# Weighted latent of an absorbed-MLA attention: plain fp32 matmuls on whole probabilities in place of three fp32r matmuls on high and low parts

## The reference, cut to what matters

```python
q_l = jnp.concatenate([qn_l, apply_axial_rope(qp_l, rope)], axis=-1)
kv = (rms_norm(c_kv, g_kva) @ w_kvup).reshape(b, t, MLA_HEADS, QK_NOPE + V_DIM)
s = jnp.einsum('bqhd,bkhd->bhqk', q, k).astype(jnp.float32) * scale
p = jax.nn.softmax(s, axis=-1).astype(v.dtype)
return jnp.einsum('bhqk,bkhd->bqhd', p, v)
```

## Time and profile before

| | |
|---|---|
| median of 3 runs | 2826.54 us (2825.86 to 2827.65) |
| time of the profiled execution | 2825.79 us |
| its span in the profile | 2823.7 us |
| TensorE busy | 2639.9 us (93%) |
| granted TensorE clock, mean | 0.972 of full speed |
| attention stage, from the first transposes to the last `weighted_values` | about 1872 to 2329 us of the span |
| one head of it | 58.3 to 58.4 us |

### The profile page before, as it was taken

One profiled execution on the slowest core, in us unless ns is written; L12 is line 12 of the kernel. 1 busy time (PEld: TensorE's weight loads), 2 busy tenths in 40 slices (PEclk: granted clock), 3 DMA queues, 4 the chain that ended last, 5 costly groups with the idle time before them and its releaser, 6 DMA issues.

```text
span 2823.7 us, 33170 instructions
## 1 busy us (share of the span) xinstructions
PE 2639.9 (93%) x12374; PEld 2131.7 (75%) x12374; DVE 1283.3 (45%) x1610; ACT 737.3 (26%) x979; POOL 638.8 (23%) x360
## 2 busy tenths in 40 slices
PE   7978888999999899999999989989999999899997
PEld 4856665777878688888888877878888887677776
DVE  5653444775123543134313565246666664522243
ACT  4133333000111222011101123146566651211120
POOL 2200110333333233333333332200000003222221
PEclk9979998999999999999999989999999999999998
DMA  4100001543112111111111111100000002000011
GB/s 149 45 27 19 30 31 47 181 167 125 46 71 82 33 52 45 52 45 49 48 64 48 52 54 38 45 23 9 7 15 7 8 9 76 30 30 30 30 41 71
DMA packets 40399, 143.27 MB, mean 51 GB/s; under 512 B 4972, under 2 KB 6252, under 8 KB 39950
## 3 DMA queue, kind: packets, MB, share of 16 engines
q1 hardware_dynamic: 35724, 124.03, 13.1%
q10 hardware_dynamic: 4610, 18.35, 1.8%
HBM read 135.81 MB, written 6.55 MB: 50 GB/s over the span
## 4 chain that ended last, share of the span: by engine, by line
PE 76%; DVE 11%; issue 6%; ACT 4%; DMA 2%; DVEq 0%; ACTq 0%; SPq 0%
PE PS L437 58%; PE PS L828 3%; PE PS L768 3%; PE PS L800 2%; PE PS L776 2%; DMA AW<-in_ada 2%; ACT E L1236 1%; PE PS L478 1%; PE PS L927 1%; PE PS L923 1%; DVE cols L1850 1%; PE PS L470 1%; DVE H L1422 1%; DVE SA L1550 1%; ACT SA L1042 1%
## 5 line engine op out<-in xcount | busy, mean ns | idle before, releaser
L437 PE MATMUL PS<-H,w_hl 128*128 128x512 f32 x6624 | 1549.6, 395 | 65.3 <-DVE H L1422 16.6
L437 PEld LDWEIGHTS PS<-H,w_hl 128*128 128x128 f32 x6624 | 1254.6, 190 | 350.9 <-issue 48.2
L412 POOL CAST w_hl<-w_raw 128x1024 fp32r<-128x1024 f32 x176 | 188.2, 1069 | 2110.9 <-PE PS L437 1697.3
L414 POOL TENSOR_TENSOR w_hl<-w_raw,w_hl 128x1024 fp32r<-128x1024 f32 x176 | 441.9, 2511 | 14.1
L437 PE MATMUL PS<-FF,w_hl 128*128 128x512 f32 x1056 | 239.8, 389 | 0.0
L437 PEld LDWEIGHTS PS<-FF,w_hl 128*128 128x128 f32 x1056 | 198.3, 188 | 41.1
L768 PE MATMUL PS<-CKV,QN 128*128 128x512 f32 (+1 forms) x576 | 146.0, 367 | 4.3 <-DVE QN L1830 4.3
L828 PE MATMUL PS<-PT,CKT 128*128 128x256 f32 x960 | 122.9, 287 | 4.1 <-DVE PT L1866 4.1
L828 PEld LDWEIGHTS PS<-PT,CKT 128*128 128x128 f32 x960 | 119.2, 194 | 8.0 <-DVE PT L1866 7.3
L1866 DVE TENSOR_TENSOR PT<-PS,PT 128x512 fp32r<-128x512 f32 (+1 forms) x192 | 103.7, 596 | 34.9 <-ACT PT L1249 34.7
L768 PEld LDWEIGHTS PS<-CKV,QN 128*128 128x128 f32 x576 | 101.2, 192 | 21.8 <-issue 4.7
(11 more groups left out here) (274 smaller groups left out, 2415.5 us busy)
## 6 DMA issues: line engine op xcount, KB each, us to landing
w_raw<-in_units SPq DMA_DIRECT2D x178, 512.0 KB, 3.5
AW<-in_ada SPq DMA_DIRECT2D x48, 512.0 KB, 3.6
X<-in_x SPq DMA_DIRECT2D x8, 512.0 KB, 7.5
XIN<-in_x ACTq DMA_DIRECT2D x8, 512.0 KB, 7.0
out<-X ACTq DMA_DIRECT2D x8, 512.0 KB, 3.0
bias_scratch<-grow ACTq DMA_DIRECT2D x4, 576.0 KB, 6.5
BR<-bias_scratch ACTq DMA_DIRECT2D x4, 512.0 KB, 3.4
CXR<-in_ctx ACTq DMA_DIRECT2D x1, 1024.0 KB, 4.8
```

Of the source, the lines that this page charges most:

```text
L412: pool.tensor_copy(hi_part, raw).then_inc(w_hi, 1)
L414: pool.tensor_tensor(lo_part, raw, hi_part.bitcast(F32), ALU.subtract).then_inc(w_split, 1)
L437: mm = pe.matmul(PS[:, out_at + a:out_at + a + m], w(s, wp, w0 + k), src[:, o:o + m], start=(k == 0 and wp == 0 and xp == 0), stop=(k == k ...
```

## The change

`PT` and `CKT` become plain fp32 tiles of half the size, each with whole numbers. `weighted_values` makes one fp32 matmul per key block in place of three fp32r ones. The evacuation of the transposes is divided between the engines: ACT copies the banks of key blocks 0 to 3 and 8, 9, DVE copies the bank of blocks 4 to 7, and no engine forms a difference. The semaphores follow: `pt_act` counts two per tile, `pt_dve` one. `CKT` is filled by ACT with the transposed high part, and DVE adds the transposed low part to it.

```diff
-    CKT = at("CKT", 2 * TK, H_AT + 22528, F32R)
+    CKT = at("CKT", TK, H_AT + 22528)
-    PT = at("PT", 2 * PTW, H_AT + 43008, F32R)
+    PT = at("PT", PTW, H_AT + 43008)
...
             elif t % 2:
-                pe.wait_ge(pt_lo, (tg - 1) * 3 + 1)
+                pe.wait_ge(pt_act, (tg - 1) * 2 + 1)
             transpose_blocks(t, 0, 4, 3072)
             transpose_blocks(t, 8, 10, 1280 + 1536 * (t % 2))
             if t % 2:
-                pe.wait_ge(pt_lo, (tg - 1) * 3 + 3)
+                pe.wait_ge(pt_dve, tg)
             else:
                 pe.wait_ge(ol_copied, h * 4 + (t // 2 + 1))
             transpose_blocks(t, 4, 8, 3584)
 
         def weighted_values(h, g):
 
-            pe.wait_ge(pt_lo, (h * 8 + (2 * g + 1)) * 3 + 3)
+            pe.wait_ge(pt_act, (h * 8 + (2 * g + 1)) * 2 + 2)
+            pe.wait_ge(pt_dve, h * 8 + (2 * g + 2))
             for kb in range(10):
-                for vp, xp in PASSES:
-                    mm = pe.matmul(PS[:, 3584:3584 + GQ], CKT[:, vp * TK + kb * P:vp * TK + (kb + 1) * P],
-                                   PT[:, xp * PTW + kb * GQ:xp * PTW + (kb + 1) * GQ],
-                                   start=(kb == 0 and vp == 0 and xp == 0), stop=(kb == 9 and vp == 1))
+                mm = pe.matmul(PS[:, 3584:3584 + GQ], CKT[:, kb * P:(kb + 1) * P], PT[:, kb * GQ:(kb + 1) * GQ],
+                               start=(kb == 0), stop=(kb == 9))
             mm.then_inc(pv_done, 1)
...
         def probs_hi(h, t):
-            for n, (k0, k1, bank) in enumerate(((0, 4, 3072), (8, 10, 1280 + 1536 * (t % 2)), (4, 8, 3584))):
+            for n, (k0, k1, bank) in enumerate(((0, 4, 3072), (8, 10, 1280 + 1536 * (t % 2)))):
                 act.wait_ge(tp_done, (h * 8 + t) * 3 + (n + 1))
-                act.activation(block_cols(0, t, k0, k1), bank_cols(bank, k0, k1), ACT.Copy).then_inc(pt_hi, 1)
+                act.activation(block_cols(0, t, k0, k1), bank_cols(bank, k0, k1), ACT.Copy).then_inc(pt_act, 1)
...
         def probs_lo(h, t):
-            for n, (k0, k1, bank) in enumerate(((0, 4, 3072), (8, 10, 1280 + 1536 * (t % 2)), (4, 8, 3584))):
-                v.wait_ge(pt_hi, (h * 8 + t) * 3 + (n + 1))
-                v.tensor_tensor(block_cols(1, t, k0, k1), bank_cols(bank, k0, k1),
-                                block_cols(0, t, k0, k1).bitcast(F32), ALU.subtract).then_inc(pt_lo, 1)
+            v.wait_ge(tp_done, (h * 8 + t) * 3 + 3)
+            v.tensor_copy(block_cols(0, t, 4, 8), bank_cols(3584, 4, 8)).then_inc(pt_dve, 1)
...
-        v.tensor_copy(CKT[:, TK:2 * TK], PS[:, 1536:1536 + TK].bitcast(F32)).then_inc(ct_lo, 1)
+        v.wait_ge(ct_hi, 1)
+        v.tensor_tensor(CKT[:, :], PS[:, 1536:1536 + TK], CKT[:, :], ALU.add).then_inc(ct_lo, 1)
```

More of the change, by code:

```diff
@@ L317, in build @@
         sem(n) for n in ("sc_done", "mx_ready", "ex_ready", "rc_ready", "e_ready"))
-    tp_done, pt_hi, pt_lo = sem("tp_done"), sem("pt_hi"), sem("pt_lo")
+    tp_done, pt_act, pt_dve = sem("tp_done"), sem("pt_act"), sem("pt_dve")
     pv_done, ol_copied, ol_hi, ol_lo = sem("pv_done"), sem("ol_copied"), sem("ol_hi"), sem("ol_lo")
@@ L782, in mla_scores @@
                 if a == 1024 and t >= 2:
-                    pe.wait_ge(pt_lo, (h * 8 + (t - 2)) * 3 + 2)
+                    pe.wait_ge(pt_act, (h * 8 + (t - 2)) * 2 + 2)
                 nope_scores(t, a, m, ends and a == 0)
@@ L855, in mla_head @@
                 if g == 1 and not last:
-                    pe.wait_ge(pt_lo, (h * 8 + 3) * 3 + 1)
+                    pe.wait_ge(pt_act, (h * 8 + 3) * 2 + 1)
                     absorb(h + 1, 1 - hh)
                 if g == 2:
-                    pe.wait_ge(pt_lo, (h * 8 + 5) * 3 + 1)
+                    pe.wait_ge(pt_act, (h * 8 + 5) * 2 + 1)
                     values(h, hh, 0)
@@ L1281, in _ @@
         act.wait_ge(ct_done, 1)
-        act.activation(CKT[:, 0:TK], PS[:, 0:TK], ACT.Copy).then_inc(ct_hi, 1)
+        act.activation(CKT[:, :], PS[:, 0:TK], ACT.Copy).then_inc(ct_hi, 1)
         rope_hi(0)
```

## The result

The changed kernel takes 2835.34 us (median of 7 runs, 2831.59 to 2838.10) against 2825.96 us for the kernel before in the same comparison (7 runs, 2824.14 to 2827.65). The ratio is 1.003, with a 95% interval of 1.0019 to 1.0042: slower by 9.4 us. Forecast were 7.5 us more and 2834.0 us, with a range of 2829.5 to 2840.0.

What follows compares the result with a forecast made beforehand. TensorE was taken to bound the attention stage, with 3.4 us idle per 58.3 us head. Six heads at +1.0 us, head 0 at +1.5 and head 7 at 0 gave +7.5 us: 2834.0 us, range 2829.5 to 2840.

Steps and rivals of the forecast that it cites:

- The price of a call: One `weighted_values` on TensorE: 20 fp32 records of 0.215 us, 4.30 us in place of 3.61, 0.69 us more.
- The rival with a surcharge per record: In `weighted_values`, changing weights lengthens each fp32 record: 4.56 us a call, total about +14 us, 2840; chance 0.09.
- its far end: Each record in `weighted_values` costs two old steps: 4.81 us a call, 2.5 us per head, 2847; within the chance of 0.09.
- Group 1 pays nothing, because the wait for `AH` covers it: weighted(1), heads 1 to 6: the longer call fits into the gap before transposes(4); 0 in place of 0.7 us.
- Tile 1 and weighted(3): Heads 1 to 6: earlier scaling regains 0.49 us at tile 1; weighted(3) loses its wait for `PT`, net +0.1 us.
- Tile 0 and `AH` stay: Heads 1 to 6: tile 0's wait stays 1.3 us, and `AH` comes when it came; the change touches neither chain.
- the rival which ended faster: Waits for tile 0 and `AH` shrink too as ACT is relieved: about -7 us, 2819; chance 0.04.
- Head 0: First head: its transposes at tile 1 show no idle time to regain, so the change costs +1.5 us.
- The end of head 7: Last head: the copies after transposes(6) and (7) are in the open; weighted(3) starts 1.65 us earlier.
- the two cases for the clock: Last call of head 7: at 1.2 GHz for 3.4 us, +0.8 us; at 2.4 GHz, -0.9 us; middle 0 taken.
- The sum: Whole kernel: +6.0 for heads 1 to 6, +1.5 head 0, 0 head 7, total +7.5 us; +5.7 to +11 had chance 0.68.
- The rival within 0.2%: Full clock in last call, gated-product wait and fewer copies at tile 0 or `AH` save time: +4.7 us, 2831.2; chance 0.19.

Runs made afterwards that it cites:

- extra_g1: Changed kernel with key block 0 multiplied and accumulated twice in the group 1 call of every head; 59.3 us a head, 2834.77 us in one run.
- evac_only: Kernel before with only the new evacuation: 30 fp32r matmuls a call kept, low part of the probabilities left out; 2815.03 us, ratio 0.9962.
- fp32_only: Kernel before with 10 plain fp32 matmuls a call, the old three copies and three subtractions kept; 2842.53 us, ratio 1.0056.
- after_ah_early: Changed kernel with ACT's `AH` copy before tile 5's exponential and DVE's low half before the reciprocal; 2828.31 us, ratio 1.0004 to the kernel before.
- one_pass: Changed kernel with `PT` and `CKT` in fp32r, 10 matmuls a call, low parts of both operands lost; 59.2 us a head, 2827.89 us in one run.
- one_pass_free: one_pass with `AH` made early and DVE's gated product and result copy ahead of the second new tile's reciprocal; 2765.67 us, ratio 0.9786 to kernel before.

## Why the prediction was right, step by step

- *The price of a call* was given as 4.30 us from 3.61, and is 4.32 us. The step was read from two records of L713 and eight of L923, and it held for 640. The rival with a surcharge per record falls with its far end: 4.56 and 4.81 us are not there. (The far end was that of the four passes in the Trainium skill, FP8 and Floating Point Precision, section TensorE Precision Notes, with an fp32r matmul counted as one pass, which was my own step; the measured call decides against 4.81 us here.)
- *Group 1 pays nothing, because the wait for `AH` covers it*: shown three times. The wait fell by the length that the call gained, a further 0.43 us in extra_g1 cost nothing, and with the wait taken away the change costs 1.7 us a head and not 1.0. The length it was to have left, about 0.6 us, is 0.56.
- *Tile 1 and weighted(3)* were to give back 0.49 and about 0.6 us; evac_only measures 1.13 us for both. *Tile 0 and `AH` stay* where ACT's and DVE's relief is concerned: evac_only keeps both at 1.3 us. That is the rival which ended faster; it falls.
- *Head 0* was to cost 1.5 us, and the step was mis-sized: it had another 0.3 us of wait in front of transposes(6), for the gated product, which the longer call also covers. From its first call to its last the changed kernel takes 0.5 us more (38.86 against 38.35), where this step gives 0.9.
- *The end of head 7*: weighted(3) was to start 1.65 us earlier relative to what precedes it. From the call of group 2 (at 2314.51 before, 2323.28 after) to the last call (2323.50 and 2331.46) it is 8.99 against 8.18 us; with 0.72 us for the longer call of group 2 in it, the gain is 1.53 us. Of the two cases for the clock, the profiled run shows the good one. The 3.4 us ahead of the last call in the kernel before, and then the rows of the changed kernel that answer to the earlier trace rows:

```profile
2320.10:2323.50 3.40, 1.49 (x11) 1.06 (x11) 3.16 (x7) 1.78 (x4) 0.00 (x0) 1.00 0.00 0
```

```profile
2328.00:2331.40 3.40, 2.21 (x18) 1.67 (x16) 1.94 (x4) 2.05 (x5) 0.00 (x0) 1.00 0.00 0
2331.40:2334.80 3.40, 3.34 (x16) 2.98 (x17) 0.00 (x0) 0.00 (x0) 0.00 (x0) 1.00 0.00 0
```

  TensorE was busy 2.21 of the 3.40 us ahead of the call and kept 2.4 GHz; in the kernel before it was busy 1.49 us of them, and the last call ran at 0.51 of the clock. From the start of the last call to `values` it is 5.98 us against 6.78, 0.8 us less where this case had 0.9. The forecast took the middle of the two cases and could not tell them apart.
- *The sum.* From the first call to `values` of head 7 the profiled executions differ by 454.46 - 448.19 = 6.3 us: 0.5 up to the last call of head 0, 5.8 in the six heads after it (6.0 in the sum), nothing behind them. The terms give 7.5 with the middle value for the clock and 6.6 with the good case.
- *The rival within 0.2%* had three parts. The good clock came, with 0.8 of its 0.9 us, in the profiled run. The wait for the gated product was there in head 0 alone (0.3 us) and not in every head, and nothing was regained at tile 0 or at `AH` (evac_only), so the other two parts fail. Yet the stage's own 6.3 us are only 0.6 us above its bound of 5.7, and the interval of the measured ratio begins at 1.0019: the mechanism of the sum is shown, but the runs are not enough to call the total clear of 0.2%.

The measured 9.4 us are more than that. The spans of the two profiles differ by 7.5 us: 6.3 in the stage, 0.9 before its first call (1882.1 and 1883.0 us) and 0.3 behind it. The 0.9 us are not the change's. L713, which runs ahead of everything in which these kernels differ, starts at 1764.1 us before and 1765.0 in the changed kernel, at 1767.8 in fp32_only and 1761.8 in after_ah_early: 6 us of scatter in a part that is the same in all of them. From there to the first call it is 118.0 us in the first three, so the new fill of `CKT` costs nothing that can be seen. That is why totals of single runs cannot tell 2.7 us apart, and why I read the size from the heads. What makes this scatter stays open: the mean granted clock of the first 550 us (0.94, 0.92, 0.94 and 0.92 in the same order) does not order the four. That the other 1.9 us, between 7.5 and the medians' 9.4, are such scatter too is argued from these numbers; no experiment isolates it. So it is partly luck that the forecast of the total came within 1.4 us of the measured median.

## What to carry to other kernels

Count the time of the steps, not the matmuls: one plain fp32 matmul of 256 columns took the time of 3.6 fp32r ones, so three split products were cheaper than one whole one, and removing copies and subtractions from idle engines paid back only the part that stood in front of a wait of TensorE. Before pricing a longer or shorter piece of work on the bounding engine, look for the wait behind it: whatever ends that wait decides whether the piece counts, and here reordering two small copies (1.4 us a head) was worth more than the whole new evacuation (1.1 us). When many matmuls are removed, new waits can take the gain back, in part by letting the clock fall: the same ten matmuls per call gave 59.2 us heads with the waits and 50.6 us heads without them, and of the 8.6 us between them 5.8 were idle time and 2.8 slower work at the lower clock.

## What the runs showed of the hardware that was not expected

- The step of fp32r matmuls of 256 columns with a new weight load each was 0.120 us, that of plain fp32 records of the same shape 0.216 us. A plain product of two records so costs 3.6 fp32r matmuls and not four. The few rows had said so; it held for 640 records.
- In one_pass, with waits of 3.7, 2.3 and 1.9 us in a head of about 60 us, the mean granted clock of a head was 0.92 to 0.94 in place of 1.00; waits of 1.3, 1.2 and 0.8 us in one_pass_free, the longest of its six, left it at 1.00.
